# Second layer's first norm: a reciprocal root in two parts, affine factors computed earlier, and low halves shared with ScalarE

## The reference, cut to what matters

```python
x = x + jnp.square(jax.nn.relu(h @ w_up[l])) @ w_down[l]      # end of the first block
...
cond = jax.nn.silu(c)
mod = cond @ mod_w[l] + mod_b[l]
shift1, scale1, gate1, shift2, scale2, gate2 = jnp.split(mod, N_MOD, axis=-1)
h = modulate(rms_norm_2(x, norm1_g[l]), shift1, scale1)       # this norm
# rms_norm_2: x * rsqrt(mean(x*x) + EPS) * g ; modulate: h * (1 + scale) + shift
```

## Time and profile before

| | |
|---|---|
| median of 3 runs | 1672.78 us (1670.04 to 1676.04) |
| the profiled execution | 1674.95 us, of which its span is 1672.7 us |
| granted TensorE clock, mean | 0.956 |
| TensorE busy | 1521.6 us, 91% of the span |
| VectorE busy | 770.4 us, 46% |
| ScalarE busy | 453.5 us, 27% |
| GpSimd busy | 589.3 us, 35% |

### The profile page before, as it was taken

The page is one execution under the profiler, slowest core; times in us unless marked ns, Lnnn a source line. Parts: engine busy times, 40 slices in busy tenths (PEclk is TensorE's granted clock), DMA queues, the critical chain, the costliest instruction groups (busy, mean ns, idle before and its releaser), DMA issues.

```text
span 1672.7 us, 21171 instructions
## 1 busy us (share of the span) xinstructions
PE 1521.6 (91%) x8338; PEld 1207.5 (72%) x8338; DVE 770.4 (46%) x1461; ACT 453.5 (27%) x714; POOL 589.3 (35%) x477
## 2 busy tenths in 40 slices
PE   6978999899999999979999999999999989986882
PEld 5877787778888888857888878775688866554541
DVE  2343756448687773245513730255313254333234
ACT  4233234333131322232323242342223121000001
POOL 2482121234554554433533244420154313222123
PEclk9988999999999999979999999999999989999896
DMA  5222010034545452213322112210033669999994
GB/s 227 76 102 76 26 51 26 26 126 188 190 177 201 156 197 101 99 58 103 108 77 97 51 51 101 100 61 26 26 151 151 254 221 376 380 395 375 398 371 163
DMA packets 36915, 256.71 MB, mean 153 GB/s; under 512 B 7232, under 2 KB 7872, under 8 KB 13008
## 3 DMA queue, kind: packets, MB, share of 16 engines
q1 hardware_dynamic: 31056, 246.94, 39.0%
q0 software_dynamic: 5760, 8.41, 1.6%
HBM read 250.59 MB, written 15.20 MB: 159 GB/s over the span
## 4 chain that ended last, share of the span: by engine, by line
PE 81%; DVE 8%; issue 4%; ACT 4%; POOL 1%; DMA 1%; SPq 0%; DVEq 0%; POOLq 0%; ACTq 0%
PE G L1981 13%; PE G L1983 12%; PE G L1982 12%; PE SA L2509 5%; PE G L2509 4%; PE SA L1981 3%; PE SA L1983 3%; PE SA L1982 3%; PE PB L1983 3%; PE PB L1982 3%; PE PB L1981 3%; PE OB L2165 2%; PE PB L2517 1%; PE G L2023 1%; PE SA L2398 1%
## 5 line engine op out<-in xcount | busy, mean ns | idle before, releaser
L712 POOL TENSOR_TENSOR wl<-raw,wh 128x512 fp32r<-128x512 f32 x364 | 487.2, 1370 | 695.1 <-ACT wh L842 695.1
L842 ACT ACTIVATE wh<-raw 128x2048 fp32r<-128x2048 f32 x91 | 174.2, 1914 | 296.5 <-PE SA L1983 152.3
L1981 PE MATMUL G<-Hh,wh 128*128 128x512 f32 x544 | 217.8, 400 | 4.9 <-DVE arena L1444 1.7
L1983 PE MATMUL G<-Hh,wl 128*128 128x512 f32 x544 | 214.0, 393 | 0.0
L1982 PE MATMUL G<-Hl,wh 128*128 128x512 f32 x544 | 214.0, 393 | 0.0
L1515 DVE SCALAR_TENSOR_TENSOR arena<-arena,st 128x256 f32<-128x256 f32 x144 | 132.9, 923 | 5.1
L1981 PEld LDWEIGHTS G<-Hh,wh 128*128 128x128 f32 x544 | 103.8, 191 | 25.9 <-issue 2.3
L1983 PEld LDWEIGHTS G<-Hh,wl 128*128 128x128 f32 x544 | 103.3, 190 | 22.6
L1982 PEld LDWEIGHTS G<-Hl,wh 128*128 128x128 f32 x544 | 103.7, 191 | 19.9
L784 POOL DMA_INDIRECT raw<-xn_rows,arena x38 | 37.1, 977 | 136.7 <-PE G L2525 111.8
L1981 PE MATMUL G<-wh,Hh 128*128 128x256 f32 x256 | 77.5, 303 | 0.5 <-DVE arena L1255 0.5
(11 more groups left out here) (474 smaller groups left out, 3129.8 us busy)
## 6 DMA issues: line engine op xcount, KB each, us to landing
raw<-in_pieces_dram SPq DMA_DIRECT2D x91, 1024.0 KB, 4.8
arena<-in_pieces_dram SPq DMA_DIRECT2D x24, 1024.0 KB, 4.8
arena<-in_wexp_dram SPq DMA_DIRECT2D x11, 2048.0 KB, 39.5
dn_w<-in_wexp_dram SPq DMA_DIRECT2D x22, 1024.0 KB, 35.3
arena<-in_wexp_dram SPq DMA_DIRECT2D x12, 1024.0 KB, 34.1
gu_y<-in_wexp_dram SPq DMA_DIRECT2D x6, 2048.0 KB, 38.5
gu_h<-in_wexp_dram SPq DMA_DIRECT2D x6, 2048.0 KB, 35.5
gu_l<-in_wexp_dram SPq DMA_DIRECT2D x6, 2048.0 KB, 35.0
```

Of the source, the lines that this page charges most:

```text
L712: ins = pool.tensor_tensor(low_[:, part], whole[:, part], high[:, part], ALU.subtract)
L842: act.activation(wh[:, split_slot(s)], wait_raw(act, sp_list[s]), ACT.Copy).then_inc(S("high_split"), 1)
L1981: pe.matmul(out, ah, bh, start=first, stop=False)
L1983: return pe.matmul(out, al, bh, start=False, stop=last)
```

## The change

Four edits meet at the second block's first norm.

1. GpSimd computes the roots of tiles 0 to 2 once ScalarE's squares are there, counts on `rstd_x`, and computes tile 3's root apart, counted on a new semaphore `rstd_tile3`. VectorE scales tile 0 after the first and tile 3 after the second.
2. VectorE's waits for `ffn_high` and `second_tables_loaded`, the zeroing of `xpad` and the factors `aff1` and `aff2` are written at another place: in the last round (r = 3) at j = 1, ahead of the four additions of groups "down" 24 to 27. A third small instruction there computes `shift_neg`, the negated shift.
3. For odd f the low half is made from a second ScalarE instruction, high half minus shift into the buffer (`htmp`), and one VectorE instruction instead of two. Even f are as before. The count `h2_high` for an odd f comes after that second ScalarE instruction.
4. The buffer, the same memory as before, is named `htmp`, and writers of its halves wait until the group two back is freed.

```diff
@@ pool: the roots
             pool.wait_ge(S("ss_x"), 3)
+            rstd_of(rstd2[:, 0:3], ms2[:, 0:3], ss2[:, 0:3], 3, D).then_inc(S("rstd_x"), 1)
             pool.wait_ge(S("ss_last"), 3)
-            rstd_of(rstd2, ms2, ss2, NT, D).then_inc(S("rstd_x"), 1)
+            rstd_of(rstd2[:, 3:4], ms2[:, 3:4], ss2[:, 3:4], 1, D).then_inc(S("rstd_tile3"), 1)
@@ act: high halves of h2
-                act.activation(Hhv[:, f, :], b[:, :], ACT.Identity, scale=aff1[:, f:f + 1], bias=modv[:, 0, f:f + 1]).then_inc(S("h2_high"), 1)
+                ins = act.activation(Hhv[:, f, :], b[:, :], ACT.Identity, scale=aff1[:, f:f + 1], bias=modv[:, 0, f:f + 1])
+                if f % 2:
+                    own(ins)
+                    if f >= 3:
+                        wait_freed(act, "h2", f - 2)
+                    ins = act.activation(htmp[:, 1, :], Hhv[:, f, :].bitcast(F32), ACT.Identity, bias=shift_neg[:, f:f + 1])
+                ins.then_inc(S("h2_high"), 1)
@@ dve: in the loop over the down pieces j of round r
                     half = j // 2
+                    if (r, j) == (FQ - 1, 1):
+                        dve.wait_ge(S("ffn_high"), 32)
+                        own(dve.memset(xpad, 0.0))
+                        dve.wait_ge(S("second_tables_loaded"), 32)
+                        wait_freed(dve, "mod", MOD_PIECES - 1)
+                        own(dve.tensor_scalar(shift_neg, modv[:, 0, :], -1.0, None, ALU.mult))
+                        own(dve.scalar_tensor_tensor(aff1, modv[:, 1, :], 1.0, cols(par, PAR2, "g_1"), ALU.add, ALU.mult))
+                        dve.scalar_tensor_tensor(aff2, modv[:, 4, :], 1.0, cols(par, PAR2, "g_2"), ALU.add, ALU.mult).then_inc(S("aff_ready"), 1)
+                        dve.wait_ge(S("aff_ready"), 1)
...
             square_last(hraw2, ss2, "down", 31)
-            dve.wait_ge(S("ffn_high"), 32)
-            own(dve.memset(xpad, 0.0))
-            dve.wait_ge(S("second_tables_loaded"), 32)
-            wait_freed(dve, "mod", MOD_PIECES - 1)
-            own(dve.scalar_tensor_tensor(aff1, modv[:, 1, :], 1.0, cols(par, PAR2, "g_1"), ALU.add, ALU.mult))
-            dve.scalar_tensor_tensor(aff2, modv[:, 4, :], 1.0, cols(par, PAR2, "g_2"), ALU.add, ALU.mult).then_inc(S("aff_ready"), 1)
-            dve.wait_ge(S("aff_ready"), 1)
-            norm_rows(2, hraw2, rstd2)
+            dve.wait_ge(S("rstd_x"), 3)
+            dve.tensor_scalar(hraw2[:, 0, :], Xv[:, 0, :], rstd2[:, 0:1], None, ALU.mult).then_inc(S("rows_normed"), 1)
+            dve.wait_ge(S("rstd_tile3"), 1)
+            dve.tensor_scalar(hraw2[:, 3, :], Xv[:, 3, :], rstd2[:, 3:4], None, ALU.mult).then_inc(S("rows_normed"), 1)
             for f in range(KT):
                 b = wait_group(dve, "h2", f)
                 dve.wait_ge(S("h2_high"), f + 1)
-                own(dve.tensor_scalar(ftmp[:, f % 2, :], b[:, :], aff1[:, f:f + 1], modv[:, 0, f:f + 1], ALU.mult, ALU.add))
-                free_group(dve.tensor_tensor(Hlv[:, f, :], ftmp[:, f % 2, :], Hhv[:, f, :].bitcast(F32), ALU.subtract), "h2", f)
+                if f % 2:
+                    ins = dve.scalar_tensor_tensor(Hlv[:, f, :], b[:, :], aff1[:, f:f + 1], htmp[:, 1, :], ALU.mult, ALU.subtract)
+                else:
...
+                    own(dve.tensor_scalar(htmp[:, 0, :], b[:, :], aff1[:, f:f + 1], modv[:, 0, f:f + 1], ALU.mult, ALU.add))
+                    ins = dve.tensor_tensor(Hlv[:, f, :], htmp[:, 0, :], Hhv[:, f, :].bitcast(F32), ALU.subtract)
+                free_group(ins, "h2", f)
```

More of the change, by code:

```diff
@@ L401, in build @@
         ss2, ms2, rstd2 = small(NT), small(NT), small(NT)
-        aff1, aff2 = small(KT), small(KT)
+        aff1, aff2, shift_neg = small(KT), small(KT), small(KT)
         ifr = small(32).rearrange("p (t n) -> p t n", t=NT)
@@ L427, in build @@
         xpad = AR(16384, 1032).rearrange("p (r n) -> p r n", r=2)
+        htmp = AR(17536, 1024).rearrange("p (r n) -> p r n", r=2)
         causal = AR(17924, 512)
@@ L1548, in _ @@
             square_last(hraw2, ss2, "down", 31)
-            dve.wait_ge(S("ffn_high"), 32)
-            own(dve.memset(xpad, 0.0))
-            dve.wait_ge(S("second_tables_loaded"), 32)
-            wait_freed(dve, "mod", MOD_PIECES - 1)
-            own(dve.scalar_tensor_tensor(aff1, modv[:, 1, :], 1.0, cols(par, PAR2, "g_1"), ALU.add, ALU.mult))
-            dve.scalar_tensor_tensor(aff2, modv[:, 4, :], 1.0, cols(par, PAR2, "g_2"), ALU.add, ALU.mult).then_inc(S("aff_ready"), 1)
-            dve.wait_ge(S("aff_ready"), 1)
-            norm_rows(2, hraw2, rstd2)
-            ftmp = AR(17536, 1024).rearrange("p (r n) -> p r n", r=2)
+            dve.wait_ge(S("rstd_x"), 3)
+            dve.tensor_scalar(hraw2[:, 0, :], Xv[:, 0, :], rstd2[:, 0:1], None, ALU.mult).then_inc(S("rows_normed"), 1)
+            dve.wait_ge(S("rstd_tile3"), 1)
+            dve.tensor_scalar(hraw2[:, 3, :], Xv[:, 3, :], rstd2[:, 3:4], None, ALU.mult).then_inc(S("rows_normed"), 1)
             for f in range(KT):
@@ L1560, in _ @@
                 dve.wait_ge(S("h2_high"), f + 1)
-                own(dve.tensor_scalar(ftmp[:, f % 2, :], b[:, :], aff1[:, f:f + 1], modv[:, 0, f:f + 1], ALU.mult, ALU.add))
-                free_group(dve.tensor_tensor(Hlv[:, f, :], ftmp[:, f % 2, :], Hhv[:, f, :].bitcast(F32), ALU.subtract), "h2", f)
+                if f % 2:
+                    ins = dve.scalar_tensor_tensor(Hlv[:, f, :], b[:, :], aff1[:, f:f + 1], htmp[:, 1, :], ALU.mult, ALU.subtract)
+                else:
+                    if f >= 2:
+                        wait_freed(dve, "h2", f - 2)
+                    own(dve.tensor_scalar(htmp[:, 0, :], b[:, :], aff1[:, f:f + 1], modv[:, 0, f:f + 1], ALU.mult, ALU.add))
+                    ins = dve.tensor_tensor(Hlv[:, f, :], htmp[:, 0, :], Hhv[:, f, :].bitcast(F32), ALU.subtract)
+                free_group(ins, "h2", f)
             wait_freed(dve, "h2", KT - 1)
```

## The result

| | before | changed |
|---|---|---|
| median (lowest to highest) | 1672.15 us (1668.42 to 1676.84) | 1677.91 us (1674.91 to 1681.79) |
| runs | 17 | 17 |
| profiled execution, its span | 1674.95, 1672.7 us | 1677.83, 1675.9 us |

The ratio of the changed kernel to the one before is 1.0029, with a 95% interval of 1.0021 to 1.0038: slower by 4.9 us (3.5 to 6.4) where the ratio is taken, and by 5.8 where the two medians are. Both stand at the edge of what the prediction calls the same: the ratio is just inside its 0.3%, the median of 1677.91 just outside its 1677.8. The forecast of 1681.2 us is 3.3 too high; the median lies in the range of 1676.0 to 1684.5.

What follows compares the result with a forecast made beforehand. TensorE was taken to bound the kernel, so an edit counts only where it moves TensorE. 8.3 + 2.4 - 1.2 - 1.5 + 0.4 = +8.4 us on the median of 1672.78 gave 1681.2 us (chance 0.66), range 1676.0 to 1684.5.

Steps and rivals of the forecast that it cites:

- stall at down piece 2: TensorE waits ahead of down piece 2 for the second table, three 128x8 instructions and one addition: +8.3 us, upper bound +8.5.
- clock after it: After the idle wait TensorE works at granted clock 0.50 for 2.8 to 5.4 us: +2.4 us, from 1.3 to 3.0.
- head: From last down addition to first transposes, the root in two parts starts the transposes earlier: -1.2 us, bounds -1.8 and -0.5.
- chain: From first transposes to first narrow product, shared odd low halves free banks sooner: -1.5 us, bounds -0.9 and -2.0.
- narrow products: They start sooner after the idle, at a clock still low: +0.4 us, bounds 0 and +1.1.
- Rival A: VectorE's small instructions slip in between GpSimd's and the clock returns after 2.8 us: +4.6 us, 1677.4; chance 0.13.
- rival D: Second table gets past the 1 MB weight piece, landing between 710.1 and 711.4: +5.9 us, 1678.7; chance 0.03.
- the removal of the block: Taking zeroing and small instructions out of the norm's start saves nothing, as they lie beside GpSimd's root: 0 us.
- price of 0.5 a pair: A pair of low halves falls from VectorE's 2.88 us to ScalarE's 2.34, the slower engine, leaving 0.5.
- Rival B: Shared low halves bring nothing and the norm's start gains only 0.5: +10.6 us, 1683.4; chance 0.13.
- the shift is passed on whole: Everything after the norm is started by TensorE or what it frees, so later stages give nothing back.
- Slower by over 0.3%: Whole kernel slower by more than 5.0 us, above 1677.8 us: chance 0.80; within 0.17, faster 0.03.

Runs made afterwards that it cites:

- stall_filled: Changed kernel plus 36 unread 128x128 by 128x512 products on TensorE ahead of down piece 2; 1676.54 us, ratio 1.0021 to before.
- root_only: Kernel before with only GpSimd's root split, tiles 0 to 2 apart from tile 3; 1673.75 us, ratio 1.0000 to before.
- root_shared_old_place: Changed kernel with zeroing, table wait and three 128x8 instructions back behind tile 3's squares; 1672.78 us, ratio 0.9997 to before.
- waits_only: Changed kernel with only zeroing and table wait at j = 1, the three 128x8 instructions back behind tile 3's squares; 1675.29 us, ratio 1.0013 to before.
- shared_only: Kernel before with only the odd low halves shared with ScalarE, and the negated shift beside the factors; 1669.36 us, ratio 0.9979 to before.
- factors_only: Kernel before with only the block of zeroing, table wait and three 128x8 instructions moved to j = 1; 1683.26 us, ratio 1.0064 to before.
- factors_j3: Changed kernel with the block of factors moved from j = 1 to j = 3, behind the additions of groups 24 to 27; 1667.63 us, ratio 0.9969 to before.
- j3_gap_filled: Kernel with the block at j = 3, plus 18 unread products on TensorE ahead of the norm's transposes; 1666.79 us, ratio 0.9963 to before.

## Why the prediction was right, and where it was off

| term | forecast | measured | by what |
|---|---|---|---|
| stall at down piece 2 | +8.3 | +8.26 | table, held small instructions, one addition |
| clock after it | +2.4 | +2.5 | 24.07 - 21.53; 2.45 by stall_filled |
| head | -1.2 | -1.5 | 4.69 - 6.17 |
| chain | -1.5 | -2.35 | 9.94 - 12.29; see below |
| narrow products | +0.4 | +0.7 | 7.51 - 6.81 |
| sum at "qk" | +8.4 | +7.7 | |
| time | +8.4 | +4.9 (3.5 to 6.4) | ratio of the runs |

The local sum came out 0.7 below the forecast, because terms missed in opposite directions: chain and head gained 1.15 more than said, the narrow products lost 0.3 more, and the stall and the clock were met.

**The stall** came out as worked out: table at 712.3 instead of 712.6, negated shift 713.68 (forecast 713.92), `aff1` 714.90 (715.17), TensorE at 716.03 (716.25). What decided was to take the table's 4.7 us and the two lengths at 371 us from rows. Rival A (the instructions slip in between) and rival D (the table gets past the weight piece) are out. The estimate that the prediction drew from the Trainium skill ("DMA: Bandwidth & Descriptors", section "Anatomy of one DMA — SWDGE (gpsimd) path"), 2.4 us, is half of the 4.6 measured for this transfer on SyncE's queue behind 1 MB; the page gives it for GpSimd's kind of transfer, and the measurement decides.

**The clock** was right with the row of a full idle followed by dense products: 5.2 slow us against 5.4 in the earlier trace rows.

**The head** was 0.3 better than said: tile 3's root ended 3.4 us after the last addition had begun (743.89 - 740.52), where 3.7 was put. The order of events was the forecast one. But what the prediction cost at nothing there, the removal of the block, is what makes edit 1 pay: GpSimd's root hid the block only as long as the root of all four tiles had to wait for tile 3. With the whole block left in its place edit 1 makes the head 2.2 to 3.4 us longer (root_only, root_shared_old_place); with only the zeroing and the wait moved it already comes out at 4.61 (waits_only). The sum was not hurt, because the edits came together; a term for edit 1 alone would have had the wrong sign.

**The chain** is the term that missed by most, 0.85 us, and in three places. First, where it ends. The prediction says "TensorE's last group of transposes opens the bank of group 4, so two and a half pairs count: 1.3". What ends the chain is the first narrow product, and it opens the bank of group 5: in the kernel before it started at 747.92, 0.11 us after the end of group 5's low half, in the changed one at 754.72, 0.17 after 754.55. Three pairs count, together 1.5 (shared_only: 1.51), so this is worth 0.2. Second, the overlap with GpSimd was put at 0.2 and is 0.6: the subtractions of groups 0 and 1 had taken 1.78 and 0.92, and now group 0's takes 1.43 and no other is held. Third, the transposes of the changed kernel start at the full clock, after the shorter gap (2.53 us for 12 instead of 2.82): 0.3, which the prediction left out. Together 2.35.

The price of 0.5 a pair was met only as a mean, and that is luck. It came from ScalarE being "the slower" at 2.34 us a pair, but no pair took that: VectorE gains 0.7 to 0.8 in the first and the third, where ScalarE's halves are ready in time, and nothing in the second, where ScalarE waits for transposes and these for a bank. Rival B, that the shared halves bring nothing, is out by shared_only.

**The narrow products** ran 4.1 slow us instead of 2.8, within the bounds.

**From +7.7 at "qk" to +4.9 in time.** In the two traces "the shift is passed on whole" held to 1328 us (+7.8). Then it shrinks, to +5.9 by 1376 us and, after swings between +2 and +7, to +3.4 at the end of the span. At 1376 us the granted clock was low in the kernel before and not in the changed one at the same work, as two windows show, first of before, then of the changed kernel:

```profile
1371.90:1375.40 3.50, 3.50 (x16) 1.83 (x16) 0.93 (x2) 0.00 (x0) 1.47 (x2) 0.51 0.30 89
```

```profile
1379.90:1383.20 3.30, 3.30 (x33) 2.16 (x32) 0.23 (x1) 0.00 (x0) 0.94 (x1) 1.00 0.20 55
```

16 products there, 33 here. Of the eleven traces three have this slow stretch: before, factors_only and root_shared_old_place; against before, the other eight gain 1.7 to 2.0 us there. The three profiled executions with it lie 2.8, 1.1 and 2.1 us above the median of their kernel's runs, those of six of the other eight below it. This speaks for a difference between executions and not for a gain that comes with the change. If so, it explains why the two traces end 3.4 us apart while the medians are 5.8 apart, but not why the time moved by less than 7.7.

Two things do repeat. Outside the span a run of before takes 2.11 to 2.25 us, and so does every run of factors_only and root_only; every run of the changed kernel and of the other kernels with edit 3 takes 1.78 to 1.93. These 0.3 us are a gain in every such run, though nothing here shows where they come from. And in nine of the ten kernels the time is below the shift at "qk", by 0.7 to 2.8 us, the tenth being factors_only. A shift at "qk" is also not always kept in the traces: factors_j3's -4.4 has become -5.9 by 771 us (granted clock 1.00 from 762.1 to 766.1 us, where the same work of the kernel before, 766.0 to 770.0, had 0.72), and stall_filled's +4.2 is +2.2 at 830 us and +6.8 at 1100. Where the other 1.6 to 2.5 us of the changed kernel go, by the medians or by the ratio, stays open.

So the forecast was 3.5 us above the measured +4.9: 0.7 is the local sum (chain and head gained more than said, the narrow products lost more), 2.8 lies behind "qk". Slower by over 0.3% had most of the chance, and by the ratio it did not happen: 4.9 us is just short of that bound of 5.0. That the time lies inside the range is owed to the width of the range as much as to the sum.

## What to carry to other kernels

Before a wait is moved forward in an engine's queue, compare two dates in the profile: when what is waited for lands, and when somebody needs the next instruction behind it; here 712.6 against 707.9, and putting the same block behind the additions made a loss of 4.9 us into a gain of 5.2. Small VectorE instructions should be priced by what GpSimd does at that moment, and an engine that is released sooner can hold another up: GpSimd's work beginning 3 us sooner made the head up to 3.4 longer. A chain over a ring of buffers ends at the bank that the next stage opens, so read which group that is.

## What the runs showed of the hardware

- A VectorE instruction on 128x8 elements took 0.17 us alone and 1.12 to 1.29 when begun beside one of GpSimd's subtractions of 128x512, in six kernels whose rows stand above, one-operand and two-operand forms alike. A row scaling of 128x1024 took 0.75 alone and 1.71 and 1.75 there. The low-half subtraction, 0.69, was held to between 0.92 and 1.78. The scaling of group 0 just ahead of it, which reads a bank of products, kept its 0.81 beside the same GpSimd work (it ended at 747.40 in the changed kernel, with GpSimd busy from 744.14), and the zeroing kept its 0.92 (root_shared_old_place).
- It works in the other direction too: GpSimd's 0.19 us instruction took 0.63 beside VectorE's row scaling, and its subtraction of 1.26 took 1.71 beside a row scaling (root_only).
- TensorE's granted clock fell 3.1 us into an idle stretch of 8.1 us and came back 5.2 us after work had begun; with 36 unread products in the stretch it never fell. In the chain of the norm, where TensorE is busy about half the time, it fell with the gap ahead of it filled (j3_gap_filled) as without.
